# Two modulation units of layer 0's first down phase moved from its start to its last blocks, and the output sent in eight transfers

## The reference

```
for each layer:
    mod = silu(c) @ w_mod + b_mod                    # 9 x 1024 values, for each stream
    x = x + 0.5 * mod[2] * swiglu(modulate(x, mod[0], mod[1]), ffn_in, ffn_out)     # gu1, down1
    x = x + mod[5] * (mixer(modulate(x, mod[3], mod[4])) @ w_out)                   # in, out
    x = x + 0.5 * mod[8] * swiglu(modulate(x, mod[6], mod[7]), ffn_in_b, ffn_out_b) # gu2, down2
```

## Time and profile before

| | us |
|---|---|
| median of 3 runs | 2617.13 |
| the runs | 2608.28, 2618.63, 2617.13 |
| the profiled execution, its own time | 2605.34 |
| its span, first to last instruction | 2603.6 |
| PE busy in it | 2473.6 (95%) |
| DVE busy in it | 1517.5 (58%) |
| ACT busy in it | 878.1 (34%) |
| mean granted TensorE clock | 0.964 of full speed |

### The profile page before, as it was taken

How to read it: one execution, slowest core, us unless ns; L and a number is a source line. 1 busy time by engine, 2 the same in 40 slices (tenths; PEclk the granted TensorE clock), 3 DMA queues, 4 the chain that set the end, 5 groups by cost and what they waited for, 6 DMA issues and landing times.

```text
span 2603.6 us, 38759 instructions
## 1 busy us (share of the span) xinstructions
PE 2473.6 (95%) x14346; PEld 2159.8 (83%) x14346; DVE 1517.5 (58%) x2434; ACT 878.1 (34%) x1066; POOL 388.1 (15%) x361
## 2 busy tenths in 40 slices
PE   6998889998999898999999999999999989998999
PEld 4998769997888787777778888878888779998999
DVE  7676657974877666245567776642222265554544
ACT  2443444444322223333232222232222242244443
POOL 0110532111011001333211111011110111001110
PEclk6999989997999999999999999999999999999999
DMA  7778544863555454211125545522222332134454
GB/s 269 264 260 292 196 154 172 273 210 120 193 193 191 154 175 168 73 61 53 49 102 204 193 177 181 166 89 97 97 82 89 113 116 80 67 113 161 161 177 162
DMA packets 79611, 400.01 MB, mean 154 GB/s; under 512 B 8688, under 2 KB 12784, under 8 KB 54320
## 3 DMA queue, kind: packets, MB, share of 16 engines
q1 hardware_dynamic: 77104, 393.39, 43.1%
q0 software_dynamic: 784, 3.15, 0.3%
q10 hardware_dynamic: 1648, 2.47, 0.3%
HBM read 396.88 MB, written 2.10 MB: 153 GB/s over the span
## 4 chain that ended last, share of the span: by engine, by line
PE 84%; DVE 7%; DMA 3%; ACT 3%; issue 2%; POOL 0%; ACTq 0%; SPq 0%; DVEq 0%; POOLq 0%
PE pg L982 24%; PE pg L984 24%; PE pg L983 24%; DMA raw<-w_t 2%; PE pg L1030 1%; PE pg L1032 1%; PE pg L1031 1%; DMA raw<-w_d 1%; DVE Yl L1785 1%; PE px L1567 1%; PE pg L1038 1%; ACT whi L601 1%; DVE TMP L1795 1%; DVE wlo L1638 1%; DVE ada L1677 1%
## 5 line engine op out<-in xcount | busy, mean ns | idle before, releaser
L982 PE MATMUL pg<-Yh,whi 128*128 128x256 f32 (+1 forms) x2784 | 950.7, 341 | 38.7 <-DVE Yl L1785 28.6
L983 PE MATMUL pg<-Yl,whi 128*128 128x256 f32 (+1 forms) x2784 | 940.1, 338 | 0.0
L984 PE MATMUL pg<-Yh,wlo 128*128 128x256 f32 (+1 forms) x2784 | 939.6, 337 | 0.0
L1643 DVE TENSOR_TENSOR wlo<-raw,whi 128x2048 fp32r<-128x2048 f32 (+1 forms) x202 | 415.0, 2054 | 536.8 <-ACT whi L606 536.1
L982 PEld LDWEIGHTS pg<-Yh,whi 128*128 128x128 f32 x2784 | 536.7, 193 | 108.0 <-issue 21.3
L984 PEld LDWEIGHTS pg<-Yh,wlo 128*128 128x128 f32 x2784 | 536.7, 193 | 53.7
L983 PEld LDWEIGHTS pg<-Yl,whi 128*128 128x128 f32 x2784 | 537.1, 193 | 52.2
L606 ACT ACTIVATE whi<-raw 128x2048 fp32r<-128x2048 f32 (+1 forms) x202 | 348.4, 1725 | 582.2 <-PE pg L984 548.2
L982 PE MATMUL pg<-Hh,whi 128*128 128x256 f32 (+1 forms) x1056 | 356.2, 337 | 12.7 <-DVE wlo L1643 7.3
L984 PE MATMUL pg<-Hh,wlo 128*128 128x256 f32 (+1 forms) x1056 | 355.0, 336 | 0.0
L983 PE MATMUL pg<-Hl,whi 128*128 128x256 f32 (+1 forms) x1056 | 354.9, 336 | 0.0
(11 more groups left out here) (285 smaller groups left out, 2379.1 us busy)
## 6 DMA issues: line engine op xcount, KB each, us to landing
raw<-w_t SPq DMA_DIRECT2D x194, 1024.0 KB, 4.8
ada<-w_ada SPq DMA_DIRECT2D x200, 512.0 KB, 3.5
raw<-w_d SPq DMA_DIRECT2D x96, 704.0 KB, 4.1
ADA<-w_ada SPq DMA_DIRECT2D x16, 512.0 KB, 16.6
NB<-na_bias POOLq DMA_DIRECT2D x8, 256.0 KB, 2.9
X<-x_t ACTq DMA_DIRECT2D x1, 1024.0 KB, 23.8
spectrum<-HF POOLq DMA_DIRECT2D x1, 1024.0 KB, 7.1
X<-ctx_t SPq DMA_DIRECT2D x1, 1024.0 KB, 7.2
```

Source lines behind the costliest of these rows:

```text
L982: pe.matmul(out, w_hi, y_hi, start=first, stop=False)
L983: pe.matmul(out, w_hi, y_lo, start=False, stop=False)
L984: return pe.matmul(out, w_lo, y_hi, start=False, stop=last)
L1643: dve.tensor_tensor(wlo[:, n % 2, 0:size], raw[:, n % 2, 0:size], whi[:, n % 2, 0:size].bitcast(F32), ALU.subtract)\
```

## The change

The two extra units of `l0_down1` keep their number but stand elsewhere. On SP they are sent behind the phase's last regular unit. On DVE the last four steps of the phase take units 12 and 13, 14 and 15, 16, and 17 in this order, where the regular spacing is one. Every unit of the phase keeps its buffer by `n % 2`, and all 216 are still computed. At the end of the program SP waits for each chunk's `dve_evac` and sends that chunk's 128 KB; `x_final` and the drain go.

```diff
@@ block.sync, load @@
                 def units(j, u):
                     for k in range(rate):
-                        unit(j * 2 * rate, ADA_BASE[name] + ADA_MORE.get(name, 0) + u * rate + k)
+                        unit(j * 2 * rate, ADA_BASE[name] + u * rate + k)
...
                 weights(0, 0)
-                for k in range(ADA_MORE.get(name, 0)):
-                    unit(0, ADA_BASE[name] + k)
                 if blocks > 2:
...
                 weights(blocks // 2 - 1, 1)
                 units(blocks // 2 - 1, 0)
                 units(blocks // 2 - 1, 1)
+                for k in range(ADA_MORE.get(name, 0)):
+                    unit(0, ADA_BASE[name] + rate * blocks + k)
...
-            sp.wait_ge(sem["x_final"], 1)
-            sp.dma_start(out_t, X[:, :, 0:256]).then_inc(sem["out_done"], 16)
-            sp.wait_ge(sem["out_done"], 16)
+            for m in range(8):
+                sp.wait_ge(sem["dve_evac"], EVAC["l1_down2"][1] + m + 1)
+                sp.dma_start(out_t[:, m, :], X[:, m, 0:256]).then_inc(sem["out_done"], 16)
+            sp.wait_ge(sem["out_done"], 8 * 16)
@@ block.vector @@
                 for k in range(rate):
-                    unit(step * rate, ADA_BASE[name] + ADA_MORE.get(name, 0) + u * rate + k, 1 if ADA_BASE[name] < 72 else 2)
+                    unit(step * rate, ADA_BASE[name] + u * rate + k, 1 if ADA_BASE[name] < 72 else 2)
+
+            def last_units(name, first, u):
+
+                more = ADA_MORE.get(name, 0)
+                for k in range(2 if u < more else 1):
+                    unit(0, ADA_BASE[name] + first + u + min(u, more) + k, 2)
@@ block.vector, ahead @@
                 base = BASE[name]
-                for k in range(ADA_MORE.get(name, 0)):
-                    unit(0, ADA_BASE[name] + k, 2)
 
                 def body(j, last):
                     for u in range(per):
-                        units(name, j * per, u)
+                        if last and name in ADA_MORE:
+                            last_units(name, j * per, u)
+                        else:
+                            units(name, j * per, u)
...
-            dve.drain().then_inc(sem["x_final"], 1)
```

## The result

| | before | with the change |
|---|---|---|
| median of 4 runs | 2615.1 us | 2599.38 us |
| the runs | 2608.28 to 2618.63 | 2598.12 to 2601.07 |
| ratio | | 0.9946, 95% interval 0.993 to 0.9961 |
| profiled execution, its own time | 2605.34 | 2601.07 |
| its span | 2603.6 | 2599.4 |

(A fourth run of the kernel before moved its median from 2617.13 to 2615.1.) The ratio is the time with the change over the time before. The kernel is 0.54% faster, by the interval 10 to 18 us. The two profiled executions are only 4.2 us apart, and the medians 15.7, where I had forecast 12.0. So the first thing to do is to find the 12 us in the traces, and then what else differs.

A forecast was written before the change was run, and what follows sets the result against it. The prediction took the kernel as bound by PE's matmuls, 84% of the span. Its terms, -9.4 + 0.1 - 2.7 = -12.0 us, taken from the median of 2617.13, gave 2605.1 us, with a range of 2594 to 2611.

The forecast's parts named there:

- The front: Start of `l0_down1`: moving two transfers and two units away removes PE's two waits and the slow clock, 9.4 us gained.
- Both readings: Two estimates for the start of `l0_down1`: direct loss of 9.5 us, and comparison with `l0_down2`, 9.49 us.
- The first wait: PE at block 1 of `l0_down1`, 4.5 us: weights sent late because of the order on SP, not bandwidth.
- The second: PE's wait at block 2 of `l0_down1`, 2.9 us: DVE late from the first delay, then extra units before the split.
- The back: End of `l0_down1`: two added units hidden by DVE's idle time, `l0_in`'s block 0 sent later; cost 0.1 us.
- my two bounds: Landing time of `l0_in`'s block 0 after sending: 4.8 us as usual, or 6.4 with the unit's 512 KB in front.
- the sign of a wrong back: Rounding of `l0_in`'s block 0 begun by a DMA, over 0.5 us late, or DVE busy up to the last addition.
- The output: Program's end: only 128 KB remains behind the last addition, landing in 2.1 us; gain 2.7, bounds 0 and 3.0.
- the rival to which I gave 0.08: End of `l1_down2`: early chunks delay block 15's weights up to 2.4 us, costing at most 1.8: 2606.9; chance 0.08.
- the range: Whole kernel's median: down to 2594 from scatter of the runs, up to 2611 from partial cases and scatter.

The follow-up runs named there:

- e4_sp_first: Kernel before, with SP sending block 1 of `l0_down1` ahead of the two extra units, DVE's order unchanged; 2604.32 us, ratio 0.9975.
- e9_out_act_b: Changed kernel with the eight output transfers on ACT's queue behind its last rounding, run again in a later series; 2594.99 us, ratio 0.9943.
- e1_front: Changed kernel with the output as before, one 1 MB transfer behind the drain, so only the units are moved; 2599.53 us, ratio 0.9957.
- e2_out: Kernel before with only the new output, eight transfers, and the units left where they stood; 2609.16 us, ratio 0.9994.
- e3_after: Changed kernel with no edit, run again beside its two halves; 2596.41 us, ratio 0.9952.
- e8_out_late: Changed kernel with the first seven output chunks held back on SP's queue until the seventh is added; 2596.13 us, ratio 0.9947.
- e10_after_b: Changed kernel with no edit, run a third time in a later series; 2597.01 us, ratio 0.9953.
- e6_late: Changed kernel with the doubled units in the last two of the four steps instead of the first two; 2610.2 us, ratio 0.9996.
- e7_out_act: Changed kernel with the eight output transfers on ACT's queue, behind its last rounding; 2595.18 us, ratio 0.9937.

## Why the prediction was right

**The front.** Predicted 9.4 us, measured 9.46 on the stretch and the same in each kernel with the move. Both readings had it: the waits and the slow clock added up gave 9.5, and the comparison with `l0_down2`, which had the new order already, 9.49. What I said of the parts was only half right. The first wait is SP's order. The second I put down to DVE's late start as well as to the extra units; in `e4_sp_first` DVE starts early and the wait is as long, but 1.52 us of it are that kernel's own, so the two shares are not told apart. The front is a chain through both engines: in the profiles SP's order alone gives 3.6 us and DVE's alone loses 57 (222.79 against 165.31 on the stretch).

**The back.** Predicted 0.1, measured 0. The block of `l0_in` landed 5.7 us after it was sent, with PE's release; my two bounds were 4.8 and 6.4. Held against the last addition, its rounding began 0 to 0.6 us late in the seven profiles with this order, and the stretch was 155.8 in all. In `e9_out_act_b`, with 0.6, no idle time is left before that addition, and the late start is more than the 0.5 us that I had named as the sign of a wrong back: the slack is as thin as it looked, and two steps later costs 10.9 us.

**The output.** Predicted 2.7 us, with 2.1 for the last chunk. It landed in 1.9 and the stretch shrank by 2.87. But the rival to which I gave 0.08, early chunks that delay the last weights, came true beside it: they were 1.0 us late, against a bound of 2.4, and PE lost 0.7 to 0.9 us at the last block, against at most 1.8. The forecast had put that at nothing. The sum of the term is 2.1 instead of 2.7.

On that rival the Trainium skill (Perfetto Trace Analysis, DMA Optimizations) had suggested different issuing engines for inputs and outputs. ACT's queue did remove the delay, but so did SP's own with later sends: later sends were enough, and no run here tries another queue with early ones. The fit in the Trainium skill (DMA: Bandwidth & Descriptors, Anatomy of one DMA), 2.0 us and the bytes, is given there for transfers that GpSimd issues; on SP's queue its 2.3 for this chunk was 0.4 above the 1.9 measured.

**The total.** -9.46 + 0 - 2.9 + 0.7 = -11.7 us, forecast -12.0. Part of that closeness is luck: the landing was 0.2 better than forecast and the back 0.1, against the 0.7 to 0.9 that I had left out. The time itself was off by 5.7 us, 2599.38 for 2605.1. I had carried over the 11.8 us between the profiled execution and a median of three runs. In the later series the kernel before had medians of 2609.71, 2611.47 and 2611.34 (23, 13 and 11 runs), 6 to 7 below that 2617.13, so the starting point was a high draw, and no mechanism stands behind it. Runs of either kernel scatter by 3 to 17 us, and the profiles show that scatter in stretches that the change does not touch; the range was wide enough for it. The forecast stood just inside 0.5% and the first measured ratio just outside it; all three ratios of the whole lie within 0.1% of the border, so on which side one falls is luck.

## What to carry to other kernels

A queue that sends weights and side work in one order makes the weights wait for whatever the side work waits for: put side loads behind the weights of the next block, and move both ends of the pair, sender and consumer, together, since one alone can cost more than both gain. Spare time on an engine is usable only in steps on which no transfer hangs; check what the last moved item releases. When stores begin while a last load is still under way, hold them back until it has landed; here that was 0.7 to 0.9 us in the profiles, too little for the runs to tell.

## What the runs showed of the hardware

A wait of 2.94 us did not lower the granted clock in the kernel before (the block behind it ran at 0.23 us a matmul from the second on), while one of 2.85 us in `e4_sp_first` was followed by 6.0 us of matmuls at 0.50, which cost some 3. The wait of 4.46 us before was followed by some 3.4 us at 0.50. Waits of the same length can cost either nothing more or as much again, and what decides stays open.

In `l1_down2`, with 256 columns a matmul, PE ran 266 or 267 matmuls in 30 us in some profiles (before, `e1_front`, `e2_out`, `e3_after`, `e8_out_late`, `e10_after_b`) and 256 to 258 in others (after, `e6_late`, `e7_out_act`, `e9_out_act_b`), busy without a gap and at full clock. A block of 33 matmuls takes 3.74 us or 3.89. The same program is in both groups (the changed kernel in after and `e3_after`), so the code does not decide it. From the first addition of that phase to the sixth it is worth 1.3 us; the cause stays open.

A 128 KB write of 1 KB rows landed in 1.9 to 2.1 us by itself and with seven sent together after the last load had landed, and in up to 4.5 when six were sent together right behind a 704 KB load, which then took 5.2 to 5.4 us instead of 4.1.
